# Forget-gate bias of an attention block: from one-hot products on TensorE to a broadcast through DRAM

## What is computed

```python
log_f = log_sigmoid(fg + b_f)                 # one value per token and head
cum = cumsum(log_f, axis=-1)                  # along the 256 tokens
s = (q @ k.T) / 8 + cum[..., :, None] - cum[..., None, :]
p = softmax(where(key <= query, s, -inf))
out = p @ v
```

## Time and profile before

| | before |
|---|---|
| median of three runs | 780.04 us (779.47 to 780.46) |
| profiled execution, first to last instruction (span) | 778.4 us |
| median of the runs less that span (start and end around it) | 1.6 us |
| PE busy | 765.5 us, 98% |
| DVE busy | 467.9 us, 60% |
| ACT busy | 393.0 us, 50% |
| POOL busy | 67.5 us, 9% |
| PE's share of the chain that ended last | 92% |
| mean granted TensorE clock | 0.997 |

### The profile page before, as it was taken

One profiled execution on the slowest core, in us unless ns is written; L12 is line 12 of the kernel. 1 busy time (PEld: TensorE's weight loads), 2 busy tenths in 40 slices (PEclk: granted clock), 3 DMA queues, 4 the chain that ended last, 5 costly groups with the idle time before them and its releaser, 6 DMA issues.

```text
span 778.4 us, 10504 instructions
## 1 busy us (share of the span) xinstructions
PE 765.5 (98%) x4081; PEld 620.9 (80%) x4081; DVE 467.9 (60%) x613; ACT 393.0 (50%) x562; POOL 67.5 (9%) x84
## 2 busy tenths in 40 slices
PE   8999999999999999999999999999999999999996
PEld 6668766778888898888788877777898888888885
DVE  3567776587766554636674435447568776545355
ACT  3447877454344343535534456666455545334363
POOL 2106121010000000002440000000010000000001
PEclk9999999999999999999999999999999999999998
DMA  9999478928676467457487535316475655553601
GB/s 290 338 347 347 163 276 323 327 75 301 239 230 202 122 220 257 167 194 251 160 296 249 194 109 192 129 59 187 138 229 165 196 183 181 198 196 128 216 27 55
DMA packets 91024, 158.71 MB, mean 204 GB/s; under 512 B 3319, under 2 KB 34259, under 8 KB 89952
## 3 DMA queue, kind: packets, MB, share of 16 engines
q1 hardware_dynamic: 88336, 151.04, 58.2%
q0 software_dynamic: 2352, 6.91, 2.9%
q10 hardware_dynamic: 288, 0.10, 0.1%
HBM read 156.95 MB, written 1.08 MB: 203 GB/s over the span
## 4 chain that ended last, share of the span: by engine, by line
PE 92%; DVE 2%; issue 1%; ACT 1%; DMA 1%; POOL 1%; POOLq 0%; SPq 0%; DVEq 0%; ACTq 0%
PE PS L1047 24%; PE PS L1049 23%; PE PS L1048 23%; PE PS L1059 6%; PE PS L1060 3%; PE PS L1265 2%; PE PS L1225 2%; PE PS L1294 1%; PE PS L1320 1%; DMA raw<-in_w_ada 1%; PE PS L1171 1%; PE PS L1069 1%; PE PS L1068 1%; PE PS L1070 1%; PE PS L1127 1%
## 5 line engine op out<-in xcount | busy, mean ns | idle before, releaser
L1659 DVE TENSOR_TENSOR wlo<-raw,whi 128x2048 fp32r<-128x2048 f32 (+3 forms) x124 | 278.4, 2249 | 144.3 <-ACT whi L1411 129.2
L1411 ACT ACTIVATE whi<-raw 128x2048 fp32r<-128x2048 f32 (+3 forms) x124 | 226.0, 1823 | 158.6 <-PE PS L1049 156.0
L1047 PE MATMUL PS<-whi,hT 128*128 128x512 f32 (+1 forms) x584 | 230.2, 394 | 2.6 <-DVE hT L1711 1.7
L1049 PE MATMUL PS<-whi,hT 128*128 128x512 f32 (+1 forms) x584 | 223.0, 382 | 0.0
L1048 PE MATMUL PS<-wlo,hT 128*128 128x512 f32 (+1 forms) x584 | 222.8, 381 | 0.0
L1047 PEld LDWEIGHTS PS<-whi,hT 128*128 128x128 f32 x584 | 109.9, 188 | 30.4 <-issue 9.8
L1049 PEld LDWEIGHTS PS<-whi,hT 128*128 128x128 f32 x584 | 109.8, 188 | 21.8
L1048 PEld LDWEIGHTS PS<-wlo,hT 128*128 128x128 f32 x584 | 110.1, 189 | 18.6
L1047 PE MATMUL PS<-whi,hidT 128*128 128x512 f32 x216 | 84.5, 391 | 0.0
L1049 PE MATMUL PS<-whi,hidT 128*128 128x512 f32 x216 | 84.1, 390 | 0.0
L1048 PE MATMUL PS<-wlo,hidT 128*128 128x512 f32 x216 | 84.1, 389 | 0.0
(11 more groups left out here) (268 smaller groups left out, 801.4 us busy)
## 6 DMA issues: line engine op xcount, KB each, us to landing
raw<-in_w_in SPq DMA_DIRECT2D x34, 1024.0 KB, 5.1
raw<-in_w_ff SPq DMA_DIRECT2D x32, 1024.0 KB, 5.4
raw<-in_w_ada SPq DMA_DIRECT2D x16, 1024.0 KB, 6.6
raw<-in_w_gate SPq DMA_DIRECT2D x10, 1024.0 KB, 5.9
raw<-in_w_up SPq DMA_DIRECT2D x10, 1024.0 KB, 5.2
raw<-in_w_down SPq DMA_DIRECT2D x10, 1024.0 KB, 5.0
raw<-in_w_ada SPq DMA_DIRECT2D x16, 512.0 KB, 8.3
raw<-in_w_out SPq DMA_DIRECT2D x8, 1024.0 KB, 5.8
```

The costliest lines, as they stand in the source:

```text
L1047: pe.matmul(o, ah, wh, start=(k == 0), stop=False)
L1049: return pe.matmul(o, al, wh, start=False, stop=end)
L1411: act.activation(split_view(whi, i)[:, c], slab_view(raw, slot, i)[:, c], ACT.Copy).then_inc(hi_made if i else part_whi, 1)
L1659: dve.tensor_tensor(split_view(wlo, i)[:, c], slab_view(raw, slot, i)[:, c], whole(split_view(whi, i))[:, c], ALU.subtract).then_inc(lo_ma ...
```

## The change

The biased mask of each fox head is built in SBUF instead. ACT writes the cumulated sum (now with a positive sign, so that nothing need be negated) from partitions 0 to 7 to a DRAM tensor `f_dram` of 8 x 384: columns 0 to 255 are all tokens, 256 to 383 the first 128 again. It waits for both writes, and then reads each pair of rows back, spread over 128 partitions, by four DMAs of 384 KB (`fcast`). POOL writes the masking value over the upper triangle of the two diagonal blocks of each head, by one affine select a unit (`fbias`). DVE uses the result as the bias of L1909. The eight products a unit, `ncum`, `identr` and the mask with its transfer (128 KB) go; the PE step `scores:0` no longer waits for the gate. The order lists of ACT and DVE change at three places.

```diff
-order += [("fgate", 0), ("unit", 0), ("unit", 1), ("logf", 0)] + early
+order += [("fgate", 0), ("unit", 0), ("unit", 1), ("logf", 0), ("fcast", 0)] + [("fbias", u) for u in range(FOX_P)] + early
 ACT_ORDER
-split:8 split:9 EV:fox0 EV:fox1 EV:fox2 split:10 fgate:0 split:11 logf:0 heads:0 split:12 heads:1 scores:0
+split:8 split:9 EV:fox0 EV:fox1 EV:fox2 fgate:0 split:10 logf:0 split:11 fcast:0 heads:0 split:12 heads:1 scores:0
 DVE_ORDER
-split:8 split:9 EV:fox0 fgate:0 EV:fox1 split:10 unit:0 unit:1 logf:0 split:11 scores:0 scores:1 probs:0
+split:8 split:9 EV:fox0 fgate:0 EV:fox1 unit:0 logf:0 split:10 unit:1 split:11 scores:0 scores:1 probs:0
 PE, scores
-                    if u == 0:
-                        pe.wait_ge(zeroed, 1)
-                        pe.wait_ge(ncum_lo, 1)
-                        for part in range(2 * picks):
-                            for n, r in enumerate(rows):
-                                pick = identr[r, n * HD + 2 * u + n:n * HD + 2 * u + n + 1].to_broadcast([HD, P])
-                                last = pe.matmul(PS[:, 5 + n, c0:c1], pick, ncum[r, part, 0:c1 - c0], start=False,
-                                                 stop=part == 1)
 ACT, logf
-                    act.activation(ncum[0:GATE, 0, :], fgt[:, 3, :], ACT.Copy, scale=-1.0).then_inc(ncum_hi, 1)
+                    act.dma_start(f_dram.ap()[:, 0:S], fgt[0:FOX, 3, :]).then_inc(f_out, 16)
+                    act.dma_start(f_dram.ap()[:, S:S + P], fgt[0:FOX, 3, 0:P]).then_inc(f_out, 16)
+                elif kind == "fcast":
+                    act.wait_ge(f_out, 32)
+                    for u in range(FOX_P):
+                        act.dma_start(fbias[:, 2 * u:2 * u + 2, :],
+                                      bass.AP(tensor=f_dram, offset=2 * u * 3 * P, ap=[[0, P], [3 * P, 2], [1, 3 * P]])
+                                      ).then_inc(fbias_in[u], 16)
 DVE, logf and scores
-                    dve.scalar_tensor_tensor(out=ncum[0:GATE, 1, :], in0=fgt[:, 3, :], scalar=-1.0,
-                                             in1=whole(ncum[0:GATE, 0, :]), op0=ALU.mult, op1=ALU.subtract
-                                             ).then_inc(ncum_lo, 1)
-                            bias = [mask[:, P:2 * P], mask]
+                            dve.wait_ge(fbias_made, u + 1)
+                            bias = [fbias[:, a, S:S + P], fbias[:, a, 0:S]]
 POOL
-            pool.memset(ncum[:, :, :].bitcast(F32), 0.0).then_inc(zeroed, 1)
-                    pool.dma_start(con[:, C_MASK:C_ALIBI], A["constants"][:, C_MASK:C_ALIBI]).then_inc(setup_in, 16)
+                elif kind == "fbias":
+                    pool.wait_ge(fbias_in[i], 16)
+                    b = fbias[:, 2 * i:2 * i + 2, P:3 * P].rearrange("p h (b k) -> p h b k", b=2)
+                    pool.affine_select(out=b, in_=b, compare_op=ALU.is_ge, fill=MASKED, base=0,
+                                       pattern=[[0, 2], [0, 2], [-1, P]], channel_multiplier=1).then_inc(fbias_made, 1)
```

More of the change, by code:

```diff
@@ L53 @@
 FF = len(FF_AT)
-STAGE = 19820
-C_ID, C_MASK, C_ALIBI, C_HOT = 0, 128, 384, 1408
+STAGE = 20204
+C_ID, C_ALIBI, C_HOT = 0, 128, 1152
 C_ALL = C_HOT + SKEW
@@ L470, in build @@
         g_dram = nc.dram_tensor("g_dram", [2, D], F32, kind="Internal")
+        f_dram = nc.dram_tensor("f_dram", [FOX, 3 * P], F32, kind="Internal")
         whi = sb("whi", [P, SPL, 4 * W], F32R)
@@ L486, in build @@
         AB = sb("AB", [P, 4, KC], F32, g)
-        wfgs = sb("wfgs", [P, 2, KC, GATE], F32R, g)
-        bf = sb("bf", [GATE, 1], F32, g)
-        fgt = sb("fgt", [GATE, 4, S], F32, g)
-        ones = sb("ones", [GATE, S], F32, g)
         valT = sb("valT", [P, S], F32, g)
-        ncum = sb("ncum", [P, 2, S], F32R, g)
         hss = sb("hss", [P, 4, TB * 8], F32, g)
@@ L496, in build @@
         drs = sb("drs", [P, TB * DIFF], F32, g)
+        gg = ExitStack()
+        wfgs = sb("wfgs", [P, 2, KC, GATE], F32R, gg)
+        bf = sb("bf", [GATE, 1], F32, gg)
+        fgt = sb("fgt", [GATE, 4, S], F32, gg)
+        ones = sb("ones", [GATE, S], F32, gg)
+        gg.close()
+        fbias = sb("fbias", [P, FOX, 3 * P], F32, g)
         od = tok1[:, 1]
@@ L574, in build @@
         con = sb("con", [P, C_ALIBI])
-        identr = sb("identr", [P, P], F32R)
         col = sb("col", [P, V_C + KC])
@@ L588, in build @@
         ident = con[:, C_ID:C_ID + P]
-        mask = con[:, C_MASK:C_MASK + 2 * P]
         raw = sb("raw", [P, RAW, 4 * W])
@@ L666, in build @@
         cum_made = sem("cum_made")
-        ncum_hi = sem("ncum_hi")
-        ncum_lo = sem("ncum_lo")
+        f_out = sem("f_out")
+        fbias_in = [sem(f"fbias_in{u}") for u in range(FOX_P)]
+        fbias_made = sem("fbias_made")
         tok_in = sem("tok_in")
@@ L914, in squares_of @@
             return (None, xnb, xnb, None, None, fin)[n][:, t, h * W:(h + 1) * W]
-        NSETUP = 6
+        NSETUP = 5
         QB = ((0, P), (P, 3 * P))
@@ L1262, in _ @@
                     for t, (c0, c1) in enumerate(QB):
-                        picks = kind_of(u) == "fox"
                         for n, r in enumerate(rows):
                             last = pe.matmul(PS[:, 5 + n, c0:c1], qT[r, slot, t * P:(t + 1) * P],
-                                             kT[r, slot, 0:c1 - c0], start=True, stop=not picks)
-                            if t == 1 and not picks:
+                                             kT[r, slot, 0:c1 - c0], start=True, stop=True)
+                            if t == 1:
                                 last.then_inc(score_ps, 1)
-                        for part in range(2 * picks):
-                            for n, r in enumerate(rows):
-                                pick = identr[r, n * HD + 2 * u + n:n * HD + 2 * u + n + 1].to_broadcast([HD, P])
-                                last = pe.matmul(PS[:, 5 + n, c0:c1], pick, ncum[r, part, 0:c1 - c0], start=False,
-                                                 stop=part == 1)
-                                if (t, part) == (1, 1):
-                                    last.then_inc(score_ps, 1)
                     for n in range(2):
@@ L1854, in _ @@
                     dve.wait_ge(fg_ps, 1)
-                    dve.tensor_scalar(fgt[:, 0, :], PS[0:GATE, 6, 0:S], bf[:, :], None, ALU.add).then_inc(fg_abs, 1)
+                    dve.tensor_scalar(fgt[:, 0, :], PS[0:GATE, 6, 0:S], bf[:, :], -1.0, ALU.add, ALU.mult
+                                      ).then_inc(fg_abs, 1)
                     dve.wait_ge(fg_abs, 1)
@@ L1863, in _ @@
                     then(dve.scalar_tensor_tensor(out=fgt[:, 2, :], in0=fgt[:, 0, :], scalar=0.0, in1=fgt[:, 1, :],
-                                                  op0=ALU.min, op1=ALU.subtract))
+                                                  op0=ALU.max, op1=ALU.add))
                     dve.tensor_tensor_scan(fgt[:, 3, :], ones[:, :], fgt[:, 2, :], 0.0, ALU.mult, ALU.add
                                            ).then_inc(cum_made, 1)
-                    dve.wait_ge(ncum_hi, 1)
-                    dve.wait_ge(cum_made, 1)
-                    dve.scalar_tensor_tensor(out=ncum[0:GATE, 1, :], in0=fgt[:, 3, :], scalar=-1.0,
-                                             in1=whole(ncum[0:GATE, 0, :]), op0=ALU.mult, op1=ALU.subtract
-                                             ).then_inc(ncum_lo, 1)
                 elif kind == "unit":
@@ L2102, in _ @@
             then(pool.memset(bf[:, :], 0.0))
-            pool.memset(ncum[:, :, :].bitcast(F32), 0.0).then_inc(zeroed, 1)
-            pool.wait_ge(zeroed, 1)
             for part in range(2):
                 pool.memset(wfgs[:, part].rearrange("p k h -> p (k h)").bitcast(F32), 0.0).then_inc(zeroed, 1)
-                pool.wait_ge(zeroed, 2 + part)
+                pool.wait_ge(zeroed, 1 + part)
             for name, r in (("fox_qk_g", V_QK), ("diff_qk_g", V_QK + 2)):
@@ L2257, in constants @@
     dist = P + np.arange(P)[:, None] - np.arange(2 * P)[None, :]
-    c[:, C_MASK:C_MASK + 2 * P] = np.where(dist >= 0, 0.0, MASKED)
     for h in range(DIFF):
```

9 lines of the change are left out of this document (2 added, 7 removed).

## The result

The changed kernel takes **783.67 us** (median of 5 runs, 783.34 to 785.01) against 780.09 us for the kernel before (5 runs, 779.47 to 780.46): a ratio of 1.0045, 95% interval 1.0034 to 1.0055. It is slower by 3.5 us, where 1.0 us less was forecast; the range, to 781.6, did not hold it. The profiled execution has a span of 781.5 us and took 783.56.

A forecast was written before the change was run, and what follows sets the result against it. PE was taken as the bound, busy 765.5 of 778.4 us. Picks of units 1 to 3 (-1.38 us) plus `scores:1` later (81.2 - 80.83) gave -1.0 us, from 780.04 to 779.0 us; range 777.4 to 781.6.

The forecast's parts named there:

- Picks and waits: On PE: dropping pick products saves 0.46 us a unit, 1.84 in four; two waits around `heads:0` save 0.5; 2.3 at most.
- fourth rival: On PE: picks not worth the computed difference, or a later wait of PE takes the gain: 780.0 us; chance 0.05.
- The cumulated sum at 70.2: Gate on ACT and DVE: sum ready at 70.2 us; ACT, after slab 10's rounding, issues the second write at 71.2.
- The write, 3.5 us: ACT's write to DRAM, issued at 71.2 under full queues, takes 3.5 us and lands at 74.7; ends 73.4 and 76.8.
- ACT's wait ahead of `heads:0`: ACT issues four reads from 74.7 to 76.3, then copies `heads:0` by 77.2; `scores:0` at about 77.2 instead of 77.56.
- The third rival: ACT, with a late write and quick reads, holds `heads:0` until 79.3; `scores:0` 1.7 us late; 780.0 us; chance 0.12.
- The first read, 4.2 us: First broadcast read, priced by the earlier `alibi` transfer, takes 4.2 us and lands at 78.9; bounds 2.2 and 6.7.
- The affine select, 0.93 us: POOL's select on 512 elements takes 0.93 us plus 0.1 hand-over; unit 0's `fbias` ready at about 79.95.
- DVE's four passes, 1.19 us: DVE needs 1.19 us for the four passes of `scores:0` before banks 5 and 6 are free for PE.
- `scores:1` at 81.2: PE begins `scores:1` at about 81.2 us against 80.83 before, after a new stall of some 1.3 us.
- Units 1 to 3 won whole: Biases of units 1 to 3 come long before they are wanted; their picks, 1.38 us, are won whole on PE.
- The second rival: Bias ready after 81.0, so PE stands at `scores:1`; 782.1 us, or 783.6 with both ends; chance 0.15.

The follow-up runs named there:

- The version with all three edits: Changed kernel with ALiBi biases issued behind the selects, `ada:9`'s megabyte held until the first read landed, and eight DRAM copies read by 16 partitions each: 779.49 us, ratio 0.9989.
- two edits of a few lines: Changed kernel with ALiBi biases issued behind the selects and `ada:9`'s megabyte held until the first read landed, still one source row: 778.92 us, ratio 0.9980.

## Why the prediction was wrong, by its steps

- **Picks and waits.** Forecast 1.84 + 0.5 = 2.3 us. Measured 2.0 without the transfers; `scores:1` takes 0.86 us as forecast (83.34 to 84.20), and `scores:0` began at 77.20 as forecast. Right but for some 0.25 us, which the wait at `heads:4` takes: that is the fourth rival's "later wait of PE", in small.
- **The cumulated sum at 70.2.** 70.2. The two writes went out at 70.23 and 70.54, not until 71.2: the first issue stands 0.6 us ahead of the end that the timeline gives to slab 10's rounding (68.93 + 1.90). Right, 0.7 on the safe side.
- **The write, 3.5 us.** 2.87 in the changed kernel; 2.9 to 4.4 over the other profiles. Right.
- **ACT's wait ahead of `heads:0`.** Reads issued from 73.43 to 75.49, `scores:0` not delayed. The third rival didn't occur; in five of the later profiles PE waited 0.16 to 0.52 us for ACT ahead of `scores:0`, the same mechanism at a third or less of the 1.7 us it was given.
- **The first read, 4.2 us: this step failed.** It took 7.60, more than the upper bound of 6.7. The row of `alibi` in the earlier trace rows was taken as the price of a transfer beside a megabyte. It isn't that. In the kernel before, `alibi` was issued 3.8 us behind the megabyte (which landed at 76.8), and when most of it moved the megabyte was through (the queues' rows from 76 to 77 us):

```profile
70.16 9.65 SPq L957 DMA_DIRECT2D raw<-in_w_ada  x2
...
73.97 0.62 POOL L2199 DMA_DIRECT2D alibi<-in_constants  x1
...
q0 software_dynamic: 91, 0.37, 91.7%
q1 hardware_dynamic: 4, 0.00, 0.2%
```

  The new read went out 0.2 us behind a megabyte and 1.2 us behind `alibi`, with both still ahead of it. The text named both neighbours and then priced the read by one of them, whose bytes had moved nearly alone. It also gave the megabyte to `ada:8`; it is `ada:9`'s.
- **The affine select, 0.93 us.** 0.64: half the elements took a third of the 1.85 us of the earlier trace rows.
- **DVE's four passes, 1.19 us.** 82.00 to 83.19. Right.
- **`scores:1` at 81.2.** 83.34, 2.1 us more: the read +3.4, its earlier issue -1.3, the select with its hand-over -0.25, DVE's start and PE's behind it +0.3.
- **Units 1 to 3 won whole.** No new gap at `scores:2` or `scores:3`, although their selects ran at 82.4 to 87.1 and not a microsecond apart. Right for units 1 and 2; of unit 3's 0.46 us, 0.18 to 0.19 was won (the wait at `heads:4`).
- **The second rival** had the mechanism: bias ready (81.83) later than its 81.0. By its own formula PE's 2.51 us less 1.38 make 781.2 us. The other 2.5 us were in no case of the prediction: 1.6 to 2.0 for the clock, and 0.3 outside the span, below. That is why the range failed and not only the forecast. That its worst case, with both ends, gives 783.6 us and 783.67 was measured is luck: there the write takes 5.5 us and `scores:1` starts 5 us late, here 2.87 and 2.51. A chance of 0.15 was too low for it, since the only two rows of a transfer to or from `g_dram` both spoke for it.

In sum, against the run without transfers: stall 3.1, clock 1.6, outside the span 0.3, together 5.0 us, less the 2.0 of gain: 3.0 us of the 3.5 measured. The rest lies within the scatter of either median.

The fit of 2.0 us and 436 GB/s, which the prediction quotes from the Trainium skill ("Anatomy of one DMA"), stands there for DMAs that GpSimd issues; these were issued by ACT. They took 2.87 us where the estimate by the fit was 2.0, and 7.60 (3.87 with both neighbours moved away) where it was 2.9.

**What stays open.** The source row. With both transfers in place, distinct rows alone brought the ratio from 1.0045 to 1.0019 and the landing 1.2 us forward, as much as either transfer. With `ada:9` held and the ALiBi biases in the way, distinct rows brought the median from 780.77 to 779.59 and copies brought it to 779.61, with intervals of the ratio that lie just apart (0.9974 to 0.9992 and 0.9976 to 0.9993 against 0.9997 to 1.0023); with the ALiBi biases away, copies brought nothing. So the two transfers are enough of a cause, but perhaps not the only one. Whether many readers of one row slow each other only beside other traffic, or the first of these differences is due to the runs that lost the clock, these runs don't tell. Nor was it tried to issue the first read alone: when it landed, ACT's queue had moved 0.8 MB in the changed kernel and 1.2 MB with `ada:9` held, two and three times its own 0.39, so that the three reads behind it may slow it as well. The version with all three edits wasn't taken apart further, nor was a direct copy from the gate's tile to the broadcast tile within SBUF tried.

## What to carry to other kernels

Before an urgent transfer is added, list what each queue has issued in the few microseconds ahead of it: its price here was its own 3.9 us plus most of what stood there, and a neighbour's duration is not its price. What is not urgent can be issued behind it, if it isn't held too long (four megabytes held cost a wait of 1.04 us): two edits of a few lines turned a loss of 0.45% into a gain of 0.20%. And a stall of TensorE is dearer than its length once the clock goes with it, so a range for a change that can make TensorE wait as long as here, some 2.4 us or more, needs that as a term of its own.

## What was not expected of the hardware

- After gaps of 3.25, 2.87, 2.38 and 2.36 us at `scores:1` the profiles show the granted clock at 0.50, for 3.4 us in three of them and 6.8 in the one with the gap of 2.87; after gaps of 2.21, 1.73 and 1.08 they show 1.00. It cost 1.6 us where it can be compared at the same start of `scores:1`.
- Outside the span, every execution with the six new DMAs takes 2.03 to 2.17 us, and every execution of the kernel before that was run beside the experiments 1.69 to 1.81; without the six DMAs it is 1.71 to 1.78, with five of them (and smaller reads) 1.90 to 1.98. So 0.3 us of the loss is in no timeline. Which property of these DMAs it is, these runs don't say.
- An affine select of 512 elements a partition took 0.64 us in all four units, against 1.85 for 1024; one of the four took 2.56 in the run that only moved the ALiBi biases.
- The issue of one broadcast read on ACT's queue took 0.36 to 0.61 us, that of a write with eight copies 0.65 to 0.75.
